# The causal mask of a stick-breaking attention stage: from a matmul on TensorE to a maximum in VectorE's running product

## The reference

```python
z = jnp.einsum('bhqd,bhkd->bhqk', q_blk, kt).astype(jnp.float32) * scale
causal = key_pos[None, :] < q_pos[:, None]
log_one_minus = jnp.where(causal, jax.nn.log_sigmoid(-z), 0.0)
log_remaining = lax.cumsum(log_one_minus, axis=3, reverse=True) - log_one_minus
weights = jnp.where(causal, jnp.exp(jax.nn.log_sigmoid(z) + log_remaining), 0.0)
return jnp.einsum('bhqk,bhkd->bhqd', weights.astype(vt.dtype), vt)
```

## Time and profile before

| | us |
|---|---|
| median of 3 runs | 2376.84 |
| lowest and highest | 2374.33 and 2377.72 |
| the profiled execution's own time | 2372.35 |
| span of its trace | 2370.5 |

### The profile page before, as it was taken

One profiled execution on the slowest core, in us unless ns is written; L12 is line 12 of the kernel. 1 busy time (PEld: TensorE's weight loads), 2 busy tenths in 40 slices (PEclk: granted clock), 3 DMA queues, 4 the chain that ended last, 5 costly groups with the idle time before them and its releaser, 6 DMA issues.

```text
span 2370.5 us, 43566 instructions
## 1 busy us (share of the span) xinstructions
PE 2273.3 (96%) x17841; PEld 2164.4 (91%) x17842; DVE 941.1 (40%) x2192; ACT 460.3 (19%) x848; POOL 225.1 (9%) x172
## 2 busy tenths in 40 slices
PE   6999999999969999999999999999999999999997
PEld 5878888777869999999999999999999999999997
DVE  6434434875363333233333333433333332333332
ACT  4243143664101111111111111111111111111110
POOL 1101101100000100001010001100010110001001
PEclk9999999999979999999999999999999999999998
DMA  4222222105378887788888877886888886888882
GB/s 163 98 71 72 89 89 65 62 2 186 114 234 265 270 284 237 236 272 268 288 277 288 278 239 248 274 278 220 289 271 283 271 265 216 286 290 272 287 271 36
DMA packets 250615, 504.05 MB, mean 213 GB/s; under 512 B 7994, under 2 KB 36718, under 8 KB 250238
## 3 DMA queue, kind: packets, MB, share of 16 engines
q1 hardware_dynamic: 234268, 451.96, 54.9%
q0 software_dynamic: 14912, 45.71, 9.7%
q10 hardware_dynamic: 1344, 5.01, 0.7%
HBM read 469.46 MB, written 31.10 MB: 211 GB/s over the span
## 4 chain that ended last, share of the span: by engine, by line
PE 91%; DVE 4%; issue 3%; DMA 1%; ACT 0%; POOL 0%; DVEq 0%; ACTq 0%; SPq 0%; POOLq 0%
PE bank L1053 43%; PE bank L1064 19%; PE bank L804 12%; PE bank L1041 3%; DVE hx L1413 2%; PE bank L1012 2%; PE bank L921 2%; PE bank L908 2%; PE bank L956 1%; PE bank L958 1%; PE bank L957 1%; PE bank L1004 1%; PE bank L886 1%; PE bank L812 1%; PE bank L898 0%
## 5 line engine op out<-in xcount | busy, mean ns | idle before, releaser
L1053 PE MATMUL bank<-hx,ring 128*128 128x140 f32 (+1 forms) x8192 | 1037.6, 288 | 26.2 <-issue 16.7
L1053 PEld LDWEIGHTS bank<-hx,ring 128*128 128x128 f32 x8192 | 1021.4, 197 | 33.2 <-issue 32.2
L1064 PE MATMUL bank<-hx,ring 128*128 128x140 f32 (+1 forms) x4096 | 514.7, 287 | 0.0
L1064 PEld LDWEIGHTS bank<-hx,ring 128*128 128x128 f32 x4096 | 507.0, 190 | 0.0
L760 ACT ACTIVATE hx<-hx 128x168 f32<-128x168 f32 x256 | 87.9, 343 | 1447.0 <-DVE hx L1484 1447.0
L1484 DVE TENSOR_SCALAR hx<-bank,hx 128x168 f32<-128x168 f32 x256 | 100.4, 392 | 639.4 <-PE bank L1053 638.9
L1509 DVE TENSOR_SCALAR hx<-bank,hx 128x168 f32<-128x168 f32 x256 | 100.5, 392 | 353.8 <-PE bank L1064 353.8
L573 POOL DMA_INDIRECT out_x<-mix,hx x66 | 99.8, 1513 | 825.4 <-ACT mix L753 780.9
L552 POOL DMA_INDIRECT mix<-xn_scratch,hx x66 | 64.7, 981 | 718.8 <-DVE hx L1408 708.7
L804 PE MATMUL bank<-hx_r,mix_r 128*128 128x512 f32 x480 | 116.1, 401 | 7.9 <-DVE hx_r L1147 7.9
L804 PEld LDWEIGHTS bank<-hx_r,mix_r 128*128 128x128 f32 x480 | 92.1, 193 | 28.4 <-issue 9.2
(11 more groups left out here) (202 smaller groups left out, 1697.8 us busy)
## 6 DMA issues: line engine op xcount, KB each, us to landing
ring<-in_w_gate_up SPq DMA_DIRECT2D x128, 2048.0 KB, 10.8
ring<-in_w_down SPq DMA_DIRECT2D x64, 2048.0 KB, 8.8
mix<-in_w_in SPq DMA_DIRECT2D x14, 1024.0 KB, 5.0
work<-in_w_in SPq DMA_DIRECT2D x14, 1024.0 KB, 5.0
ring<-in_x SPq DMA_DIRECT2D x8, 512.0 KB, 8.2
hx<-in_w_out SPq DMA_DIRECT2D x1, 4096.0 KB, 14.1
work<-in_x ACTq DMA_DIRECT2D x8, 512.0 KB, 4.8
out_x<-work SPq DMA_DIRECT2D x8, 512.0 KB, 4.4
```

The lines of the kernel that those rows point to most:

```text
L1053: mm = e.matmul(bank[f % 2][:, part * CAP:part * CAP + w], gu_ring[:, k, f * 256 + part:(f + 1) * 256:2], xT[:, k, 0:w], start=k == 0, sto ...
L1064: return e.matmul(bank[2 + j % 2][:, 0:w], dn_ring[:, k, j * P:(j + 1) * P], hid[:, k, 0:w], start=k == 0, stop=k == KD - 1)
```

## The change

The mask matmul and its two constant tiles go. The constant tile of 0 and -1e30 becomes one of 0 and 1, with 1 where the key is not before the query. A strip `past` of 512 columns holds zeros and, in its last 128 columns, this tile. The scan of a diagonal unit has so far been state = (stick * state) * 1. It becomes state = max(stick * state, past), with the last `w` columns of the strip read backwards. Where the strip is 1, the state stays 1, whatever the score was; past the diagonal the strip is 0, and the maximum leaves the product as it is. Scans of other units stay as they were. VectorE now fills the strip with a memset and a copy and waits for both before its first scan; TensorE's wait for the constants goes. The third matmul of the scores now ends the group and signals in all units.

```diff
-            e.wait_ge(z_const, 2)
...
                 for m, pr in heads:
-                    mm = e.matmul(bank[m % 4][:, 0:u["w"]], q_lo[pr, p, queries], k_hi[b][pr, keys], start=False,
-                                  stop=not u["diag"], skip_group_check=True)
-                    if not u["diag"]:
-                        mm.then_inc(z_ok, 1)
-                if u["diag"]:
-                    for m, pr in heads:
-                        e.matmul(bank[m % 4][:, u["w"] - P:u["w"]], ident_r, mask_r, start=False, stop=True,
-                                 skip_group_check=True).then_inc(z_ok, 1)
+                    e.matmul(bank[m % 4][:, 0:u["w"]], q_lo[pr, p, queries], k_hi[b][pr, keys], start=False,
+                             stop=True, skip_group_check=True).then_inc(z_ok, 1)
...
                     left = 1.0
+                    least, with_least = past[:, CH - u["w"]:][:, ::-1], ALU.max
                 else:
                     e.wait_ge(z_rem, n - 1)
                     left = rem[:, u["row"], u["at"] + u["w"]:u["at"] + u["w"] + 1]
+                    least, with_least = ones[:, 0:1].to_broadcast([P, u["w"]]), ALU.mult
                 e.tensor_tensor_scan(rem[:, u["row"], u["at"]:u["at"] + u["w"]][:, ::-1], stick[:, n % 4, 0:u["w"]][:, ::-1],
-                                     ones[:, 0:1].to_broadcast([P, u["w"]]), left, ALU.mult, ALU.mult).then_inc(z_rem, 1)
+                                     least, left, ALU.mult, with_least).then_inc(z_rem, 1)
...
-            e.tensor_copy(ident_r, ident).then_inc(z_const, 1)
-            e.tensor_copy(mask_r, mask_bias).then_inc(z_const, 1)
+            e.memset(past[:, 0:CH - P], 0.0).then_inc(z_const, 1)
+            e.tensor_copy(past[:, CH - P:CH], no_key).then_inc(z_const, 1)
+            e.wait_ge(z_const, 2)
```

More of the change, by code:

```diff
@@ L59 @@
 EPS = 1e-6
-BIG = 1.0e30
 GLIM = 7.0
@@ L83, in constants @@
     t[:, C_ID:C_ID + P] = r == c
-    t[:, C_MB:C_MB + P] = np.where(r <= c, -BIG, 0.0)
+    t[:, C_MB:C_MB + P] = np.where(r <= c, 1.0, 0.0)
     t[:, C_BO:C_BO + P] = (r // HD) == (c // HD)
@@ L134, in layer @@
         ident = cst[:, C_ID:C_ID + P]
-        mask_bias = cst[:, C_MB:C_MB + P]
+        no_key = cst[:, C_MB:C_MB + P]
         block_ones = cst[:, C_BO:C_BO + P]
@@ L189, in layer @@
         dv = region(ring, 3072, NT, CH)
-        ident_r = region(ring_r, 128, P)
-        mask_r = region(ring_r, 256, P)
+        past = region(ring, 256, CH)
         q_hi = [region(ring_r, at, S) for at in (8192, 1024)]
```

## The result

| | before | after |
|---|---|---|
| median of 6 runs | 2375.59 us | 2355.53 us |
| lowest and highest | 2370.44 and 2377.72 | 2351.78 and 2357.80 |
| profiled execution, its span | 2372.35, 2370.5 | 2354.11, 2352.3 |

The ratio is 0.9921, with a 95% interval of 0.9907 to 0.9935: 19 us less by the ratio (20.1 us between the two medians), where 8.3 had been forecast and 10.9 was the end of the range. The direction was right, the size was not.

The account below looks back on a forecast made before the run. TensorE was taken to bound the stage: 25 twos of masks at 0.37 us, 9.25, less 0.9 for ScalarE waits, gave 8.35 us; 2376.84 - 8.3 = 2368.5 us, range 2366.0 to 2374.3.

Parts of the forecast that it names:

- TensorE set the pace: Stick-breaking stage, each head-pair period: TensorE busy 31.15 us, falling to 28.19 without masks, against 25.14 for VectorE.
- Two masks: Diagonal steps on TensorE: removing two mask matmuls saves 0.37 us; 25 such twos count, 9.25 us.
- their gap: TensorE's mask slot, taken to close; rival: it does not, masks worth 80 ns each, 2373.7 us, chance 0.17.
- The scan: VectorE's diagonal scans: maximum and strip add zero; rivals: dearer by half, chance 0.06, by more, 0.06.
- Three waits for ScalarE: TensorE's scores wait 0.1 us at three places per period, 0.9 us altogether; rival: 0.37 us each, 2370.9 us, chance 0.15.
- the masks under the stop: Five twos of masks before TensorE's standstill until 412.45 us, waiting for POOL: removing them gains nothing.
- the last copy: End of the stick-breaking stage: its last copy comes at about 527.4 us instead of 535.67.
- The three repeating periods: Head pairs after the first: 24 of the 25 counted twos of masks; each period about 28.5 us, from 31.15.
- TensorE's first values: Early in the stage, line 921 still starts first at about 412.4 us, after TensorE's wait for POOL.
- No DMA, loop or stop after it is tied to an absolute time: After the stick-breaking stage: whatever the stage wins, the whole kernel wins; clock shifts allowed 1.5 us either way.
- The first head pair: Start of the stage: of three twos of masks after the stop, only the one at 431.06 us counts.
- VectorE's dense stretch: First head pair, 420.25 to 436.4 us without a gap: it doesn't start sooner, so two waits eat two masks.

Follow-up runs that it names:

- e10: Against the kernel before: maxima only in the first ten units, all other masks on TensorE, expert loop kept where it stood; 2373.5 us, ratio 1.0005.
- e8: Against the kernel before: mask matmuls in the first head pair alone, maxima in the other three, expert loop kept where it stood; 2365.8 us, ratio 0.9967.
- e1: Changed kernel plus 64 unread small transposes on TensorE ahead of the expert loop, putting it back where it stood before; 2363.5 us, 0.9951 of the kernel before.
- the twins with one width: Kernel before and changed kernel, each with one width (168 tokens) for all experts, so the loop has one body; 2580.8 and 2568.8 us.
- e12: Changed kernel plus 16 unread matmuls of 512 columns in TensorE's stop ahead of its first values; 2357.0 us, 0.9931 of the kernel before.
- e15: Changed kernel with TensorE waiting for the two constants at the stage's start again; 2355.5 us, 0.9934 of the kernel before.
- e9: Against the kernel before: maxima in the first head pair alone, mask matmuls in the other three, expert loop kept where it stood; 2372.2 us, ratio 0.9995.
- e2: Kernel before plus 64 unread small transposes on TensorE ahead of the expert loop, masks unchanged; 2366.7 us, ratio 0.9972.

## Why the prediction was right and wrong

**Right, by its own steps.** TensorE set the pace, and VectorE stayed under it (24.86 us busy in 28.58). Two masks were worth 0.37 us, and their gap closed in full. The scan cost the same to the hundredth of a us. Three waits for ScalarE in a period took 8 x 0.37 - 2.58 = 0.38 us where 0.3 had been put, and the masks under the stop were worth nothing that could be seen (e10). In the profiled pair the last copy came at 527.66 us; 527.4 was forecast. That this fits so well is in part luck: 0.7 us of it is an earlier start, and the pair sets the shortest stage with masks against the longest of six without. The three repeating periods gave 7.8 us in the timed run (e8) and 7.7 by the traces. TensorE's first values came at 411.76 and not at 412.4. The likely reason is that POOL's first subtraction had hardly a scan beside it; the sum had left that out, and it is 0.7 us.

**The step that failed.** It was "No DMA, loop or stop after it is tied to an absolute time, so what the stage wins, the kernel wins." I asked whether the time of the loop could matter and not whether its place in the program could. Taking 128 instructions out of TensorE's program moved the expert loop by half a block of fetched instructions. That is worth 7 us in either direction: 0.9951 against 0.9921 in the changed kernel, 1 against 0.9972 in the kernel before (0.28 to 0.30%), with no change to the work. It could have been seen before: the trace of before shows the second stops of TensorE in three items (0.92, 0.75 and 2.39 us), released by "issue", in a loop that the change moves. I had looked only at the stage.

**A term that was mis-sized.** The first head pair had one two of masks in the sum. The stage as a whole gained 10.8 us in the mean of the traces and 11.6 (e1 against before) or 12.1 us (the twins with one width) in the timed runs, where 8.35 had been put. The periods are as forecast, so by the traces the missing 2.5 to 3.5 us lie in the first pair. (The timed runs that split the masks add up to 7.8 + 1.2 = 9.0 us, within their intervals of either sum.) I had read that pair from one execution, which was the shortest of five, and had argued that VectorE's dense stretch would keep its place and hold the gain back; it began at 419.02 us in the changed kernel and not at 420.25. Part of the shortfall goes with the granted clock, 0.83 to 0.87 in most executions with masks. Why the clock falls more often there is open: filling TensorE's stop did not raise it in the changed kernel (e12), the wait for the constants did not lower it in e15, and in e9 it was low with no mask matmul in the first pair.

**The sum in hindsight.** About 11 us for the masks and 7 for the place of the loop make 18, against 19 by the ratio. With both kernels at places of one kind, the change measures 11.6 us (e1 against before); with the kernel before at the good place and the changed one at the bad, 5 us (e1 against e2, 0.9951 and 0.9972).

## What to carry to other kernels

Where a program has a loop with branches in it, count the instructions that a change adds or removes ahead of the loop, per engine, and look for stops at "issue" behind a branch. Here the place of the loop's bodies against the blocks of 256 instructions was worth 7 us, more than half of what the change itself was worth. To measure a change by itself, fill its program up to the old length, as e1 does, or compare both kernels without the branch. And read a term that is to carry a sum from more than one execution where the clock is not at 1.00.

## What the runs showed of the hardware that was not expected

- A switch between two bodies of TensorE's loop stops TensorE for 1.9 to 2.6 us (items 13, 17 and 24), with a second stop for 0.75 to 3.6 us more, often with a stretch at 1.2 GHz behind it. 64 useless transposes made a kernel of 2374 us faster by 0.28%.
- A running product with a maximum against a strip that is read backwards from memory takes the same 2.34 us for two scans of 128x512 as one with a broadcast 1.
- While POOL subtracts tiles of 128x512, two scans of that size on VectorE take 4.45 us where they take 2.46 without it. The changed kernel's timeline, with POOL at work and later without:

```profile
419.02 4.45 DVE L1268 TENSOR_TENSOR_SCAN work<-work,cst 128x512 f32<-128x512 f32 x2
...
436.77 2.46 DVE L1268 TENSOR_TENSOR_SCAN work<-work,cst 128x512 f32<-128x512 f32 x2 [0.54 <-ACT work L688]
```
